# One block for the token mixing and the feed-forward of a hybrid decoder layer

## The reference, cut to what matters

```python
h   = rms_norm(x, g_pre_mix)
rq, rk, rv, rg, aq, ak, av = split(h @ w_in)
ret = group_norm(retention(rq, rk, rv)) * silu(rg)
att = dilated_attention(aq, ak, av)
mix = concat([ret, att]) @ w_out
x   = x + rms_norm(mix, g_post_mix)
h   = rms_norm(x, g_pre_ffn)
f   = (silu(h @ w_gate) * (h @ w_up)) @ w_down
x   = x + rms_norm(f, g_post_ffn)
```

## Time and profile before

| | |
|---|---|
| time of three runs, median (lowest to highest) | 2703.97 us (2700.41 to 2704.01) |
| time of the profiled execution | 2700.68 us |
| its span, first to last instruction | 2698.5 us |
| TensorE busy | 2530.2 us, 94% of the span |
| VectorE, ScalarE, GpSimd busy | 48%, 33%, 24% |
| mean granted TensorE clock | 0.97 of full |

### The profile page before, as it was taken

How to read it: one execution, slowest core, us unless ns; L and a number is a source line. 1 busy time by engine, 2 the same in 40 slices (tenths; PEclk the granted TensorE clock), 3 DMA queues, 4 the chain that set the end, 5 groups by cost and what they waited for, 6 DMA issues and landing times.

```text
span 2698.5 us, 36922 instructions
## 1 busy us (share of the span) xinstructions
PE 2530.2 (94%) x12568; PEld 2126.0 (79%) x12568; DVE 1306.8 (48%) x2493; ACT 898.8 (33%) x1779; POOL 640.8 (24%) x405
## 2 busy tenths in 40 slices
PE   6999998999989889998399999979999999999998
PEld 5888887789988857876388888768888878888886
DVE  5213455425655577875665666675656542101001
ACT  4112111136766623332344444444444431100000
POOL 1794544322444077774000000000000000000000
PEclk9999999999999989999699999989999999999999
DMA  4322223364436245553333332433332336424242
GB/s 169 96 75 65 74 101 117 113 174 136 108 102 184 72 131 167 171 168 100 124 121 120 109 117 98 143 113 121 105 120 92 122 129 209 173 94 161 99 154 102
DMA packets 247322, 333.72 MB, mean 124 GB/s; under 512 B 17456, under 2 KB 153392, under 8 KB 246960
## 3 DMA queue, kind: packets, MB, share of 16 engines
q1 hardware_dynamic: 247216, 332.34, 38.1%
HBM read 214.44 MB, written 117.83 MB: 123 GB/s over the span
## 4 chain that ended last, share of the span: by engine, by line
PE 47%; DVE 3%; issue 1%; DMA 1%; ACT 0%; POOL 0%; SPq 0%; POOLq 0%; DVEq 0%
PE ff_psum_bank L1527 30%; PE ff_psum_bank L1595 17%; DVE ff_b_lo L1775 1%; DMA ff_b<-h 0%; DVE ff_total L1921 0%; DVE ff_total L1925 0%; DMA ff_x<-x 0%; POOL ff_ssq L1765 0%; DVE ff_sums L1790 0%; DVE ff_b_sum L1806 0%; DVE ff_b_sum L1799 0%; DVE ff_b_sum L1813 0%; DMA ff_acts<-a_lo 0%; ACT ff_squares L1750 0%; DVE ff_w_lo L1771 0%
## 5 line engine op out<-in xcount | busy, mean ns | idle before, releaser
L1527 PE MATMUL ff_psum_bank<-ff_b_hi,ff_w_hi 128*128 128x512 f32 x1232 | 486.4, 395 | 54.6 <-DVE ff_b_lo L1775 34.5
L364 PE MATMUL pr_psum_acc<-pr_hT_hi,pr_weights 128*128 128x512 f32 x1536 | 482.2, 393 | 12.0 <-DVE pr_weights L271 12.0
L1527 PE MATMUL ff_psum_bank<-ff_b_lo,ff_w_hi 128*128 128x512 f32 x1232 | 484.6, 393 | 0.0
L1527 PE MATMUL ff_psum_bank<-ff_b_hi,ff_w_lo 128*128 128x512 f32 x1232 | 484.4, 393 | 0.0
L1595 PE MATMUL ff_psum_bank<-ff_down_hi,ff_acts 128*128 128x512 f32 x1408 | 438.0, 392 | 9.9 <-DVE ff_down_lo L1908 4.5
L364 PEld LDWEIGHTS pr_psum_acc<-pr_hT_hi,pr_weights 128*128 128x128 f32 x1536 | 291.2, 190 | 75.1 <-issue 13.1
L1595 PEld LDWEIGHTS ff_psum_bank<-ff_down_hi,ff_acts 128*128 128x128 f32 x1408 | 266.4, 189 | 67.9 <-issue 8.9
L1527 PEld LDWEIGHTS ff_psum_bank<-ff_b_hi,ff_w_hi 128*128 128x128 f32 x1232 | 234.6, 190 | 108.0 <-DVE ff_b_lo L1775 37.0
L364 PE MATMUL pr_psum_acc<-pr_hT_lo,pr_weights 128*128 128x512 f32 x768 | 301.1, 392 | 0.0
L1595 PE MATMUL ff_psum_bank<-ff_down_lo,ff_acts 128*128 128x512 f32 x704 | 275.6, 391 | 0.0
L1527 PEld LDWEIGHTS ff_psum_bank<-ff_b_lo,ff_w_hi 128*128 128x128 f32 x1232 | 234.8, 191 | 48.9
(11 more groups left out here) (170 smaller groups left out, 3746.6 us busy)
## 6 DMA issues: line engine op xcount, KB each, us to landing
ff_raw<-in_w_gate SPq DMA_DIRECT2D x22, 1024.0 KB, 6.5
ff_raw<-in_w_up SPq DMA_DIRECT2D x22, 1024.0 KB, 5.4
a_hi<-ff_a_hi SPq DMA_DIRECT2D x88, 256.0 KB, 2.0
...
```

The source lines that it names most:

```text
L364: last = nc.tensor.matmul(acc[:, bank, :], w[:, s, k, :], h[:, k, t], start=k == 0 and n == 0, stop=k == KT - 1 and n == 2)
L1527: last = nc.tensor.matmul(to, w[:, i, k, :], b[:, i, k, :], start=fresh and k == 0 and which == 0, stop=k == KH - 1 and which == 2, skip_g ...
```

## The change: one block, frames in common, and a new order where the stages meet

Mix and feed-forward become functions that give out their engine programs, and one block calls them one after the other; the barrier between them is gone, with the final waits of mix on its stores. Both stages take their SBUF from one map of 22 frames of 8192 bytes per partition, and all eight PSUM banks from one allocation, so that each buffer of the feed-forward lies where mix has ended its use, and waits on mix's semaphores guard it. The identity matrix, which mix loaded again, is kept from the stages before. Step 18 is no longer a step of mix. What it held is spread over the feed-forward's first tile.

```diff
+        mixed = mix(nc, D, w_out, first["ident"], bank, spent)
+        fed = ffn(nc, D, bank, mixed)
+        with nc.Block() as block:
...
-            for c in range(LAST, CHUNKS + LAG_H):
+        for c in range(LAST, CHUNKS + LAG_H - 1):
             step(c, c % 2, lambda lag, c=c: 0 <= c - lag < CHUNKS)
+            if then is not None:
+                then(c)
...
+    def load_early(sp, c):
+        if c == CHUNKS - 2:
+            sp.wait_ge(mixed["h_stored"], 16 * CHUNKS // HALVES)
+            load_b(sp, 0, 0)
+            load_raw(sp, "w_gate", 0, 0)
+        elif c == CHUNKS - 1:
+            sp.wait_ge(S["kv_done"], CHUNKS)
+            for q in (2, 3, 1):
+                load_b(sp, 0, q)
...
+        mixed["store_x1"](sp, CHUNKS - 1)
+        sp.wait_ge(S["x_sq"], CHUNKS)
+        load_raw(sp, "w_up", 0, 1)
+        mixed["store_h"](sp, CHUNKS - 1)
...
+    def round_early(act, c):
+        if c == CHUNKS:
+            act.wait_ge(S["att_done"], CHUNKS)
+            high(act, P1, 0, 0)
+            high_b(act, P1, 0)
+            high(act, P2, 0, 0)
+        elif c == CHUNKS + 1:
+            act.wait_ge(S["lo_b"], CHUNKS)
+            high_b(act, P2, 0)
+            for i in (P6, P5, P7):
+                high(act, i, 0, 0)
...
+        def first_turn():
+            act.wait_ge(done[P1], 1)
+            act.wait_ge(S["y_scaled"], 2 * CHUNKS)
+            snap(0, 0)
+            high_b(act, P5, 0)
+            mixed["square_x"](act, CHUNKS - 1)
+            act.wait_ge(done[P6], 1)
+            act.wait_ge(S["h2_done"], CHUNKS)
+            snap(1, 0)
+            high(act, P1, 1, 1)
+            mixed["copy_h"](act, CHUNKS - 1)
+            high_b(act, P7, 0)
+            high_b(act, P4, 0)
+            high(act, P4, 0, 0)
...
+    def sum_early(dve, c):
+        if c == CHUNKS:
+            low(dve, P1, 0, 0)
+            first_sum(dve, 0)
+            add_weights(dve, 0, 0)
+        elif c == CHUNKS + 1:
+            low_b(dve, P1, 0)
+            dve.wait_ge(S["y_done"], CHUNKS - 1)
+            third_sum(dve, 0)
+            low(dve, P2, 0, 0)
+            low_b(dve, P2, 0)
+            low(dve, P6, 0, 0)
...
+            if isinstance(n, int) and n == 0:
+                mixed["turn_h"](pe, CHUNKS - 1)
```

More of the change, by code:

```diff
@@ new lines, in ffn @@
+    acts = [place(f"acts{n}", [P, 2, GROUP], frame((15, 11)[n // 2], n % 2 * 4096), F32R) for n in range(4)]
+    gain = place("gain", [P, DM], WIDE + 36864)
+    x1 = [place("x1_0", [P, DM], WIDE + 24576), place("x1_1", [P, DM], WIDE + 40960)]
+    squares = place("squares", [P, GROUP], WIDE + 45056)
+    total = place("total", [P, 2, DM], frame(10))
+    ssq = place("ssq", [P, 2, 2], NARROW)
+    minus_half = place("minus_half", [P, 1], NARROW + 32)
+    X, Y, Z = ([bank[:, n, :] for n in two] for two in ((2, 5), (3, 0), (4, 1)))
@@ new lines, in started, with weight, load_raw @@
+    def started(n):
+        return not isinstance(n, int) or n > 0
+    def weight(i, s):
+        near, far = slice(0, KH), slice(KH, KT)
+        return {P1: raw[s][:, near, 0:P], P2: raw[s][:, far, 0:P], P6: sums[:, s, 1], P5: sums[:, s, 0],
+                P7: raw[s][:, near, P:PW], P4: raw[s][:, far, P:PW], P3: sums[:, s, 2]}[i]
+    def load_raw(sp, name, j, s):
+        src = D[name][:, bass.ts(j, PW)].rearrange("(k p) n -> p k n", p=P)
+        sp.dma_start(raw[s][:], src).then_inc(raw_loaded[s], 16)
@@ new lines, in low, with low_b, add_weights @@
+    def low(dve, i, n, s):
+        dve.wait_ge(w_hi_done[i], n + 1)
+        nc.vector.tensor_tensor(w_lo[:, i], weight(i, s), w_hi[:, i].bitcast(F32), ALU.subtract).then_inc(w_lo_done[i], 1)
+    def low_b(dve, i, half):
+        dve.wait_ge(b_hi_done, NP * half + i + 1)
+        nc.vector.tensor_tensor(b_lo[i][:], b22[:] if i == P3 else b_sum[i][:], b_hi[i][:].bitcast(F32),
+                                ALU.subtract).then_inc(b_lo_done, 1)
+    def add_weights(dve, n, s):
+        old = {i: weight(i, s) for i in range(NP)}
+        dve.wait_ge(raw_loaded[s], 8 * (n - s) + 16)
+        nc.vector.tensor_tensor(old[P5], old[P7], old[P4], ALU.add).then_inc(sums_done, 1)
+        dve.wait_ge(sums_done, 4 * n + 1)
+        nc.vector.tensor_tensor(old[P7], old[P1], old[P7], ALU.subtract).then_inc(sums_done, 1)
+        nc.vector.tensor_tensor(old[P6], old[P5], old[P1], ALU.subtract).then_inc(sums_done, 1)
+        dve.wait_ge(sums_done, 4 * n + 3)
+        nc.vector.tensor_tensor(old[P3], old[P2], old[P6], ALU.subtract).then_inc(sums_done, 1)
```

1995 lines of the change are left out of this document (1008 added, 987 removed).

## The result

| | before | after |
|---|---|---|
| time, median of 4 runs, us | 2703.56 (2700.41 to 2704.01) | 2660.12 (2654.30 to 2662.52) |
| profiled execution, its time and its span, us | 2700.68, 2698.5 | 2661.69, 2659.8 |
| mean granted clock over the span | 0.970 | 0.977 |

The ratio is 0.9838, 95% interval [0.9825, 0.9852]: faster by 43 us. The prediction said 2666, range 2655 to 2682. The direction and the range held. The sum under it forecast a gain of 36.5 us where the medians show 43.4; the seam gave 38.2 of it, and another place, which the sum left out, 3.8.

What follows compares the result with a forecast made beforehand. TensorE's chain bounds the kernel, idling in the 62.7 us seam before its unbroken run. Seam after: 1.6 + 18.9 + 5.7 = 26.2, gain 36.5; 2664.2 from the profiled execution, 2667.5 from the median; predicted 2666, range 2655 to 2682.

Steps and rivals of the forecast that it cites:

- Last `w_out` matmul late: Mix steps 16 and 17: VectorE's added splitting and sums make mix's last matmul end at 1279.6, 1.6 us lost.
- The first step of the queueing: Step 16: chunk 14's `y_mean` queues behind VectorE's added sums and comes 1.0 us late; TensorE waits for it.
- the second step: Step 17: the second sum delays `h2` of chunk 14 to 1273.0; TensorE, done at 1272.5, waits 0.6 us.
- L to P7: From the last `w_out` matmul's end, 1279.6, to the start of tile 0's product P7, 1298.5: 18.9 us.
- Given back: Before P7 of tile 1: tile 2's late weight block idles TensorE 3.3 us, low clock adds 2.4; 5.7 lost.
- The clock's 2.4: After the idle before P7 of tile 1, TensorE runs one product of 12 matmuls at low clock: 2.4 us more.
- That cost cancels: At P7 of tile 0: TensorE probably starts at the low clock after 5.3 us idle, as before after 8.4.
- The seam in all: Between mix and feed-forward: 62.7 us before, 26.2 after, counting the late matmul and the time given back; gain 36.5.
- The clause on the exclusive lock: P7's difference moved from GpSimd to VectorE: costs 2.2 us instead of 4.4; all `add_weights` instructions stay under 0.7.
- 1358 us less 5 or so behind P7 as before: Sign in the profile after: from P7 to the end stays as before, 1358 us less 5 or so.
- The hidden block: Rival: tile 2's late weight block costs nothing before P7 of tile 1; gain 42, 2658 to 2662 us; chance 0.16.
- the third: Rival, more late: 5.04 us sum returns, both mix gaps run slow, weight blocks land late; 2670 to 2682; chance 0.21.

Runs made afterwards that it cites:

- The layers: Against the kernel before: one block alone, 0.9964; early loads as well, 0.9915; early splits too, chunk 15 ahead of the tiles, 0.9866; the whole change, 0.9823.
- the last version: Changed kernel with weight sums in VectorE's idle time, P3 and P4 split early, P7's operand taken out of chunk 15's chain: 2649.12 us, ratio 0.9789.
- the two versions where nothing slow follows P7's wait: One block alone with loads, splits and chunk 15 in the old order, 2694.89 us; the same with early loads, 2683.53 us.
- the second profile with the old seam: Kernel before with one edit: each last activation tile of a down projection round is waited for in the first bank's turn; 2699.72 us, ratio 0.9976.
- the two other groups: Unaltered changed kernel run again beside other experiments: 2658.69 us, ratio 0.9823, with the layered versions; 2655.93 us, ratio 0.9825, as control in the third group.

## Why the prediction was right, and by how much each term was off

- **Last `w_out` matmul late: forecast 1.6, measured 2.5.** The first step of the queueing was as forecast, TensorE's wait 3.31 instead of 2.48. What I had at nothing was the clock behind that wait: starts are 0.43 apart at 1274.61 and 1275.04, 1.7 us in all. It took the place of the second step, the 0.6 us wait for `h2` of chunk 14: TensorE ends its half at 1279.97, when `h2` has been ready since 1278.63, and waits for nothing. That it was VectorE's sums is shown by the version that moves them away (2.5 back). The bound that the text gave, L later than 1282, was written as a clock time of one execution; L came at 1286.3 because S came at 1253.05. Counted from S the bound is 34.7 us and L comes at 33.2, 0.9 over the forecast.
- **L to P7: forecast 18.9, measured 18.5** in all three executions of the change, with the wait before P6 (1.7 forecast, 1.07 measured) and before P7 (5.3 and 5.24) where they were put. The last link came out as forecast: rounding behind the copy of `h`, then the low part. Not as forecast was what leads to it. I followed VectorE's queue from the work put into steps 16 and 17, "no slack from 1259 to 1299". But VectorE waits 0.42 us for chunk 15's sum of squares (1287.06, 0.8 behind L, where I had 1.3; that is the shorter wait before P6), and from there the chain is chunk 15's `x1`, P6's low part, P6, P5, transposes, copy, rounding, low part. So L to P7 is 18.4 or 18.5 also where L comes 2.5 earlier or 4.7 later. That the sum over VectorE's queue came to nearly the same length was luck in part: in the forecast that queue ended only 0.5 us behind chunk 15's square (1280.9 against 1280.4). The layers show that each of loads, splits and place of chunk 15 is needed for it, and the last version shows that the operand's place behind the copy held P7: moved ahead of it, L to P7 is 14.15.
- **Given back: forecast 5.7, measured 3.5** (409.2 against 405.7). The wait before P7 of tile 1 was 2.8 where I had 3.3, behind the same DMA, issued 10.1 us behind P7 (10.5 forecast). The clock's 2.4 was sized too high: 1.7 behind that wait. 1776 matmuls in a row cost 402.9 by the last version's rate (383.85 / 1692 = 0.2269 each), and as much in the two versions where nothing slow follows P7's wait; so before had 2.8 on top for the low clock behind its wait for P7, and after 6.2, for one wait and two stretches at the low clock. "That cost cancels" didn't hold: 2.8 before, 1.7 after. Against the second profile with the old seam, where it was 1.3, the term is 4.9. The version that splits the weights early sheds 3.7 of them.
- **The seam in all:** 26.2 forecast, 24.5 measured; gain 36.5 forecast, 38.2 measured, or 36.8 against the second profile with the old seam.
- **The clause on the exclusive lock held.** All `add_weights` instructions take 0.68 to 0.69 us in the kernel after, where the earlier trace rows had one of 5.04:

```profile
L1858 DVE TENSOR_TENSOR ff_sums<-ff_sums,ff_raw x44: 681/683/689, 1269.6 to 2126.0; 128x512 f32<-128x512 f32 x44
```

  Putting the difference back on GpSimd brought the loss back at once, to another instruction with both inputs in SBUF: 5.62 us against 1.28, ending 1.09 behind GpSimd's end. The Trainium skill, "SBUF — State Buffer", section "Who interferes with whom", says that the two engines contend only over a port pair that they share, that it is an exclusive lock, and that a VectorE instruction with two SBUF inputs contends with a GpSimd instruction that reads SBUF. These rows agree.
- **What failed: "1358 us less 5 or so behind P7 as before".** The clause doesn't fit its own sum, which puts 5.7 us on top of the 1357.8 of before: 1363.5. Measured from P7 to the end are 1355.0, 8.5 less; 2.2 of that is the term above, the rest lies behind R. I took everything there as unchanged. I had read the diff's re-indented down projection as only re-indented. Its moved wait is worth 3.8 us in the last round, shown from both sides. The rest of the 6.2 by which R to the end is shorter (2.4 us) lies in the second half's run (405.4 against 404.2) and the down projection's first rounds. The change itself had 405.7 for that run in its second profile, and 379.7 for those rounds where before has 379.3 and its own first profile 378.1. So this rest is no more than the spread between executions of one kernel.
- **The median of before lay 3 us over its profiled execution.** So 2664.2 was the sum's value against one execution and 2667.5 against the median. With the 1.7 of the seam and the 3.8 of the last round the latter is 2662.0, against 2660.1 measured, and 2655.9 and 2658.7 in the two other groups.
- **Rivals.** The hidden block did not come by itself: the DMA was there and late. Of the third only the low clock behind one wait in mix came. The loads were in time: no wait for a load in steps 16 and 17. Over the whole span the clock rose, 0.970 to 0.977.
